# A hybrid decoder step in compensated matmuls: dense operands streamed backwards, and feature tiles at shifted addresses

## What is computed

```python
h = rmsnorm(x, norm_mix)
z = h @ w_in                     # one projection, 2048 -> 129 blocks of columns, split among the mixers
o_a = dsa_attention(...); o_b = moba_attention(...); o_c = retention(...)
m = sigmoid(g_a) * (o_a @ w_pa) + sigmoid(g_b) * (o_b @ w_pb) + sigmoid(g_c) * (o_c @ w_pc)
x = x + m @ w_out
# the ConvFFN; D_FF = 5504, 43 tiles of 128 features
u = h2 @ ffn_up;  g = h2 @ ffn_gate          # h2 = rmsnorm(x, norm_ffn)
c = conv_b + sum_j conv_w[j] * ext[:, j:j + t]
y = (gelu(c) * g) @ ffn_down
x = x + y
```

## Time and profile before

| | |
|---|---|
| median of 2 runs | 2369.28 us (2369.23 to 2369.33) |
| profiled execution, first to last instruction | 2368.6 us |
| outside the span, against the median | 0.7 us |
| TensorE busy | 2354.7 us, 99% of the span |
| share of L803 in the chain that ended last | 88% |
| granted TensorE clock, mean | 0.997 of full speed |

### The profile page before, as it was taken

One profiled execution on the slowest core, in us unless ns is written; L12 is line 12 of the kernel. 1 busy time (PEld: TensorE's weight loads), 2 busy tenths in 40 slices (PEclk: granted clock), 3 DMA queues, 4 the chain that ended last, 5 costly groups with the idle time before them and its releaser, 6 DMA issues.

```text
span 2368.6 us, 44628 instructions
## 1 busy us (share of the span) xinstructions
PE 2354.7 (99%) x17242; PEld 2273.6 (96%) x17242; DVE 1407.6 (59%) x2107; ACT 919.6 (39%) x1283; POOL 312.1 (13%) x629
## 2 busy tenths in 40 slices
PE   9999999999999999999999999999999999999998
PEld 9978999999999999999999999999999999999998
DVE  6535568899897545445456645666654456666433
ACT  5334343433433444334333344333333333333432
POOL 1135110000002222333200011000000000000000
PEclk9999999999999999999999999999999999999998
DMA  8448645556658988999776544444445544444553
GB/s 245 147 133 246 176 145 181 176 173 206 207 174 263 310 293 290 300 338 312 239 262 201 184 152 151 152 153 151 152 150 152 154 152 157 154 150 152 155 149 114
DMA packets 176307, 458.70 MB, mean 194 GB/s; under 512 B 25226, under 2 KB 75002, under 8 KB 175968
## 3 DMA queue, kind: packets, MB, share of 16 engines
q1 hardware_dynamic: 142192, 370.84, 48.8%
q0 software_dynamic: 26128, 75.67, 10.0%
q10 hardware_dynamic: 7776, 9.35, 1.1%
HBM read 425.27 MB, written 27.52 MB: 191 GB/s over the span
## 4 chain that ended last, share of the span: by engine, by line
PE 96%; DVE 1%; ACT 1%; issue 1%; DMA 1%; SPq 0%; DVEq 0%; ACTq 0%
PE ps L803 88%; PE ps L1077 1%; PE ps L1030 1%; PE ps L876 1%; PE ps L1060 1%; DMA w_raw<-in_w_in 1%; PE ps L1000 0%; ACT w_hi L1129 0%; PE ps L943 0%; PE ps L992 0%; PE ps L888 0%; PE ps L983 0%; PE ps L979 0%; DVE w_lo L1406 0%; PE ps L840 0%
## 5 line engine op out<-in xcount | busy, mean ns | idle before, releaser
L1406 DVE TENSOR_TENSOR w_lo<-w_raw,w_hi 128x1024 fp32r<-128x1024 f32 (+2 forms) x630 | 750.7, 1194 | 776.4 <-ACT w_hi L1129 773.1
L803 PE MATMUL ps<-h_hi,w_hi 128*128 128x320 f32 x3696 | 1160.4, 314 | 2.2 <-DVE h_lo L1569 1.7
L803 PE MATMUL ps<-h_lo,w_hi 128*128 128x320 f32 x3696 | 1131.6, 306 | 0.0
L803 PE MATMUL ps<-h_hi,w_lo 128*128 128x320 f32 x3696 | 1125.1, 304 | 0.0
L1129 ACT ACTIVATE w_hi<-w_raw 128x1024 fp32r<-128x1024 f32 (+2 forms) x630 | 649.3, 1033 | 804.8 <-PE ps L803 776.1
L803 PEld LDWEIGHTS ps<-h_hi,w_hi 128*128 128x128 f32 x3696 | 694.0, 188 | 33.0 <-issue 28.1
L803 PEld LDWEIGHTS ps<-h_lo,w_hi 128*128 128x128 f32 x3696 | 694.2, 188 | 0.5
L803 PEld LDWEIGHTS ps<-h_hi,w_lo 128*128 128x128 f32 x3696 | 693.8, 188 | 0.0
L803 PE MATMUL ps<-y_hi,w_hi 128*128 128x320 f32 x688 | 213.3, 310 | 0.0
L803 PE MATMUL ps<-y_lo,w_hi 128*128 128x320 f32 x688 | 210.5, 306 | 0.0
L803 PE MATMUL ps<-y_hi,w_lo 128*128 128x320 f32 x688 | 209.2, 304 | 0.0
(11 more groups left out here) (329 smaller groups left out, 2069.9 us busy)
## 6 DMA issues: line engine op xcount, KB each, us to landing
w_raw<-in_w_in SPq DMA_DIRECT2D x250, 512.0 KB, 5.0
w_raw<-in_ffn_up SPq DMA_DIRECT2D x86, 512.0 KB, 3.9
w_raw<-in_ffn_gate SPq DMA_DIRECT2D x86, 512.0 KB, 3.8
w_raw<-in_ffn_down SPq DMA_DIRECT2D x80, 448.0 KB, 3.4
kpg<-in_cache_b_k SPq DMA_DIRECT2D x128, 128.0 KB, 4.6
vpg<-in_cache_b_v POOLq DMA_DIRECT2D x128, 128.0 KB, 5.1
kpg<-in_cache_a_k SPq DMA_DIRECT2D x128, 128.0 KB, 4.8
vpg<-in_cache_a_v POOLq DMA_DIRECT2D x128, 128.0 KB, 5.0
```

The lines of the kernel that those rows point to most:

```text
L803: mm = mmul(bank[q][:, 0:T], wp[:, s, cols], xp[:, x.k0 + k, :], start=(x.first and k == 0 and t == 0), stop=(x.last and k == x.nk - 1 and ...
L1406: tt(w_lo[:, s, 0:n], w_raw[:, s, 0:n], w_hi[:, s, 0:n].bitcast(F32), ALU.subtract).then_inc(w_lo_done, 1)
```

## The change

Two edits. First, all dense matmuls of L803 read their moving tile from the last token to the first, and write their PSUM columns in the same order, from 319 to 0. Each token's result still lands in its own column. The weights' operand is as it was. Second, the tiles of `y_hi` lie 326 values apart (1304 bytes) and those of `y_lo` 330 (1320 bytes), and in the second half of the ConvFFN a tile starts 2 values later (`y_hi`) or 4 values later (`y_lo`) in its place. So the start of a feature tile, taken modulo a small power of two, changes from tile to tile. `y_lo` begins 544 bytes further on. No instruction is added, removed or moved on any engine; the same names with the same counts stand in the same order, and only addresses and steps of operands differ.

```diff
-        y_hi = at(0, 28160)("y_hi", [P, KF1, T], F32R)
-        y_lo = at(28160, 56320)("y_lo", [P, KF1, T], F32R)
+        y_hi = at(0, 28704)("y_hi", [P, KF1, T + 6], F32R)
+        y_lo = at(28704, 57760)("y_lo", [P, KF1, T + 10], F32R)
...
-             "m": (m_hi, m_lo), "y": (y_hi, y_lo)}
+             "m": (m_hi, m_lo)}
+
+        def feature(n):
+
+            i, late = n % KF1, n // KF1
+            return y_hi[:, i, 2 * late:2 * late + T], y_lo[:, i, 4 * late:4 * late + T]
+
+        def moving(job, k):
+            if job.src == "y":
+                return feature(job.wk + k)
+            xh, xl = X[job.src]
+            return xh[:, k, :], xl[:, k, :]
...
-                    xh, xl = X[job.src]
                     for k in range(x.nk):
+                        xh, xl = moving(job, x.k0 + k)
...
-                            mm = mmul(bank[q][:, 0:T], wp[:, s, cols], xp[:, x.k0 + k, :],
+                            mm = mmul(bank[q][:, 0:T][:, ::-1], wp[:, s, cols], xp[:, ::-1],
...
-                    fn(y_hi[:, job.n % KF1, :], yt[:, job.n % 2, :], ACT.Copy).then_inc(rounded, 1)
+                    fn(feature(job.n)[0], yt[:, job.n % 2, :], ACT.Copy).then_inc(rounded, 1)
...
-                    i = n % KF1
-                    tt(y_lo[:, i, :], yt[:, n % 2, :], y_hi[:, i, :].bitcast(F32), ALU.subtract).then_inc(split, 1)
+                    y_h, y_l = feature(n)
+                    tt(y_l, yt[:, n % 2, :], y_h.bitcast(F32), ALU.subtract).then_inc(split, 1)
```

## The result

The changed kernel takes 2408.15 us (2407.81 to 2408.5, 2 runs) against 2369.28: 38.9 us more, a ratio of 1.0163 with a 95% interval of 1.0146 to 1.018. It is slower, clear of noise, by less than 2%.

A forecast was written before the change was run, and what follows sets the result against it. The pace of one dense matmul, 144.45 ns times 14688, was taken to bound the kernel. Span 2368.6 us plus zero for all three terms plus 0.7 us outside gave 2369.3 us; range 2280 to 2455 us, chance 0.82.

The forecast's parts named there:

- "I take zero" for the backward walk: All 14688 dense matmuls: reading moving tile and writing PSUM backwards costs nothing; bounds inside a triple 65 us won, 82 lost.
- rival C: Dense matmuls: clash of weight load and moving stream gets worse, every distance at least the long one; 2451 us, chance 0.10.
- the all-short bound of A: Dense matmuls: all distances in a triple become the short 0.14 us, 4.45 ns x 14688 = 65 us won, 2304 us.
- Rival A: Dense matmuls: the 11.1 ns excess shrinks as direction and addresses change the clash with weight loads; 2304 or 2260 us, chance 0.24.
- Rival B: Dense matmuls: PSUM or moving read serves descending columns singly, at half rate; 126.9 ns each, 4233 us, chance 0.13.
- Rival D: Dense matmuls: the build puts both reversed patterns back in ascending order, so no operand turns; forecast time, within its 0.53.
- The feature tiles: The 2064 matmuls on `y`: new tile addresses cost zero, between 9 us won and 11 us lost.
- The writers: ScalarE's copy and VectorE's subtraction writing feature tiles: zero; if odd starts doubled them, 20 and 21 us, hidden by dense stream.

The follow-up runs named there:

- the benches: The dense matmul by itself, the layer's computation left out, at varied offsets of tiles and weights; forwards 144.4 ns over whole triples at the kernel's own offsets.
- the read alone: Kernel before with only the moving tile read backwards, PSUM written forwards, so tokens come out mirrored: 2408.19 us, ratio 1.0157.
- the last corner: Kernel before with moving tile and PSUM columns reversed and two 32-byte fillers moved ahead of the weights, feature tiles where they were: 2398.32 us, ratio 1.0123.
- the first bench: Dense matmul by itself in stretches of 48, varying columns, offsets and direction; 64 pairs of weight offsets gave 144.4 to 148.9 ns forwards.

## Why the prediction came out as it did

**The bound** was right: the pace of one dense matmul, at 14.7 us a nanosecond. 38.9 us over 14688 are 2.6 ns. All other engines and queues followed.

**"I take zero" for the backward walk** is the step that failed. It measured 33.7 us (reversal alone), 2.3 ns a matmul. That the time lies in the stated range and within 2% is luck: the forecast's own range, 2358 to 2380, doesn't hold it. The stated range reached to 2455 for the sake of rival C, and it is C's mechanism, at less than half its price, that came. C gave 82 us, from the longest distance of a triple read as 0.15 us off a row with two decimals. By the single starts of that trace the distances were 148.3, 143.3 and 141.7 ns. With these C's price would have been 3.9 x 14688 = 57 us, or 2426 us, and the all-short bound of A 2.8 x 14688 = 41 us instead of 65. The reversed `h` triples that take 443.3 ns have distances of 149.2, 147.9 and 146.2, near to C's picture of all at the longest; those at 440.0 have three alike.

The reason for the zero was weak, and the profile could have told so. The excess was "the same for sources that lie at different addresses", so it was taken for a property of the instructions. But every moving tile of the kernel before starts at the same offset modulo 256 bytes from the weights. Rows from places that are alike in the one thing that matters say nothing of it.

**Rival A** had the right parts (the weight load and the stream meet; direction and address decide) and the wrong sign. The forward kernel already stands at the best that the benches found in steps of 16 bytes, 144.4 ns over whole triples. Its 11.1 ns above the columns are no reserve that these offsets can win.

**Rival B**, half rate, is out, and with it the strict reading of the Trainium skill's rule. "PSUM — Partial Sum Buffer" of the Trainium skill says that a non-contiguous pattern slows matmuls significantly; for a step of -1 over a contiguous run it costs nothing, 2369.15 against 2369.21 us. Rival D is out as well, since the build did turn the operands.

**The other rule that was weighed**, two read ports for TensorE so that a weight load takes nothing from the running matmul ("TensorE: Matmul & The Clock Gate" of the Trainium skill, step 1, LDWEIGHTS), doesn't describe these runs. Moving the weights by 32 and 64 bytes, with nothing else changed, cost 28 us.

**The feature tiles** were bounded at -9 to +11 us and taken at zero, for the same weak reason. Alone they cost 7.3 us. On top of the reversal they added 5.3 us between medians (2408.15 and 2402.87), but that can't be told from which of the two patterns the other matmuls are in: between the trace of the changed kernel and that of the reversal alone the long piece differs by 0.05 us, features 2.3 us slower in the former (446.7 against 443.3 ns a triple), `h` about as much faster (441.7 against 443.3). The match of 908.01 and 907.96 us is thus a coincidence.

**The writers** kept their durations, and the term was rightly zero.

**What stays open.** The runs show that the distance between tile and weights decides the pace, and the direction of the read with it. That it is the weights' load beside the stream that meets the read follows from this, since in the bench nothing else reads the weights; but no run left the loads out, and how the memory decides it cycle by cycle isn't shown. Nor is it shown what puts a reversed kernel into its 440 or its 443.3 ns pattern. In the changed kernel the triples on `m` and the first 15 on `h2` are at 440.0; behind two other matmuls the next 687 are at 443.3, and after the first half's features the 671 of the second half are at 440.0 again. If a whole run were in the one or the other, 3.3 ns x 4896 = 16 us would lie between. That this makes the wider spread of the reversed kernels (2401.88 to 2408.52 for the read alone) fits the last corner, which stays at 440.0, at 2398.32 us with a spread of 1.7, but the traces are of single executions and don't show it.

## What to carry to other kernels

When back-to-back float32r matmuls with a weight load each set the time, as here, the distance in memory between the moving tiles and the weights is a tuning knob of a few per cent: 1.2% in this kernel, and 144.4 to 148.9 ns between offsets of the first bench. Edits that look harmless (a filler, another array ahead, a padded tile) can turn it. Keep the starts of all moving tiles alike modulo 256 bytes and search the offset of the weights against them, forwards at 320 columns; at another width measure both directions, since at 288 backwards was the faster. Before taking "it is the same everywhere in this trace" as evidence, check that the cases differ in the thing in question.

## What the runs showed of the hardware that was not expected

- With 320 columns, reading the moving operand backwards was in none of 256 places as fast as the best forward offset: 146.6 ns against 144.4. With 288 columns it was 2.2 ns faster than forwards at the one offset that ran.
- Writing PSUM backwards costs nothing: 887.50 us for the long piece either way.
- Paces cluster: 433.3, 440.0 and 443.3 ns a triple, and a pattern, once entered, lasts over hundreds of matmuls.
- With the weights at offset 0, a tile start 4 bytes off costs 4.6 ns forwards (151.3 against 146.7), and 12 bytes off costs 6.6 backwards (153.3) and nothing forwards.
- 128 and 192 float32r columns with a weight load beside each take the same 111.7 ns; at 320, 384, 448 and 512 columns the excess over one column in 1/2.4 ns is 8.3 to 8.5%.
